# Second-half router logits taken from raw residual chunks, rows finished on three engines, one-step SiLU gate

## The reference, cut to what matters

```
x = x + g1 * mixed
h2 = rms_norm(x, norm2_g) * (1 + sc2) + sh2
g_logits = hf @ w_rg + b_rg                       # 4 groups
e_logits = (hf @ w_re + b_re)                     # 32 experts, hf = h2 in f32
... top-1 group, top-2 experts in it, softmax gates
(jax.nn.silu(xb @ w1[e]) * (xb @ w3[e])) @ w2[e]  # per expert, rows gathered from h2
x = x + g2 * y;  y = rms_norm(x, final_norm_g)
```

## Time and profile before

| what | value |
|---|---|
| median of 3 runs | 1680.51 us (1679.48 to 1683.24) |
| the profiled execution's own time | 1682.7 us |
| its span, first to last instruction | 1680.9 us |
| PE busy | 95% of the span |
| DVE busy / ACT busy | 75% / 48% |

### The profile page before, as it was taken

One profiled execution on the slowest core, in us unless ns is written; L12 is line 12 of the kernel. 1 busy time (PEld: TensorE's weight loads), 2 busy tenths in 40 slices (PEclk: granted clock), 3 DMA queues, 4 the chain that ended last, 5 costly groups with the idle time before them and its releaser, 6 DMA issues.

```text
span 1680.9 us, 23712 instructions
## 1 busy us (share of the span) xinstructions
PE 1600.2 (95%) x9358; PEld 1377.5 (82%) x9358; DVE 1262.6 (75%) x1699; ACT 804.7 (48%) x875; POOL 235.1 (14%) x231
## 2 busy tenths in 40 slices
PE   5999999999999999999999988999999999999953
PEld 3777788788789999999999987888888888888841
DVE  4668886746838798877444268989999899899838
ACT  4222232234333213222242444878878878788723
POOL 0310000000000000002001111354321211212100
PEclk9999999999999999999999998999999999999977
DMA  9955222424434232234223457999999999999855
GB/s 338 305 179 175 83 86 83 139 76 147 120 101 151 88 88 70 76 94 133 70 82 112 184 200 225 415 390 402 385 379 377 375 381 380 379 386 397 300 220 198
DMA packets 215761, 368.51 MB, mean 219 GB/s; under 512 B 15110, under 2 KB 163654, under 8 KB 190298
## 3 DMA queue, kind: packets, MB, share of 16 engines
q1 hardware_dynamic: 197724, 327.95, 55.3%
q0 software_dynamic: 17280, 36.89, 6.1%
q10 hardware_dynamic: 646, 2.15, 0.3%
HBM read 353.45 MB, written 31.20 MB: 229 GB/s over the span
## 4 chain that ended last, share of the span: by engine, by line
PE 86%; DVE 7%; DMA 2%; DVEq 2%; ACT 1%; issue 1%; SPq 1%; POOLq 0%; ACTq 0%
PE z L2426 15%; PE z L2428 15%; PE z L2427 15%; PE z L723 7%; PE z L725 7%; PE z L724 7%; PE z L740 4%; PE z L741 4%; PE z L742 4%; PE q L714 2%; PE q L2319 1%; DMA w_raw<-in_w_in_dram 1%; PE q L731 1%; SPq L1226 1%; DVE conv L1917 1%
## 5 line engine op out<-in xcount | busy, mean ns | idle before, releaser
L970 DVE TENSOR_TENSOR wl<-wr,whr 128x2048 fp32r<-128x2048 f32 x198 | 444.3, 2285 | 0.0
L2426 PE MATMUL z<-h_hi,w_hi 128*128 128x272 f32 (+1 forms) x1248 | 410.6, 329 | 2.1 <-DVE h_lo L1740 1.2
L2428 PE MATMUL z<-h_hi,w_lo 128*128 128x272 f32 (+1 forms) x1248 | 404.9, 324 | 0.0
L2427 PE MATMUL z<-h_lo,w_hi 128*128 128x272 f32 (+1 forms) x1248 | 404.5, 324 | 0.0
L878 ACT ACTIVATE whr<-wr 128x2048 fp32r<-128x2048 f32 x198 | 376.4, 1914 | 35.8 <-PE z L725 31.5
L1740 DVE TENSOR_TENSOR w_lo<-w_raw,w_hi 128x1024 fp32r<-128x1024 f32 (+1 forms) x168 | 179.5, 1069 | 139.4 <-ACT w_hi L1472 139.4
L2426 PEld LDWEIGHTS z<-h_hi,w_hi 128*128 128x128 f32 x1248 | 236.7, 190 | 31.4 <-issue 12.4
L2428 PEld LDWEIGHTS z<-h_hi,w_lo 128*128 128x128 f32 x1248 | 236.4, 189 | 17.3
L2427 PEld LDWEIGHTS z<-h_lo,w_hi 128*128 128x128 f32 x1248 | 236.8, 190 | 15.9 <-issue 0.2
L723 PE MATMUL z<-whr,xTh 128*128 128x512 f32 x528 | 210.0, 398 | 2.4 <-DVE xTl L970 2.4
L725 PE MATMUL z<-wl,xTh 128*128 128x512 f32 x528 | 207.1, 392 | 0.0
(11 more groups left out here) (378 smaller groups left out, 2216.0 us busy)
## 6 DMA issues: line engine op xcount, KB each, us to landing
wr<-in_w_dram SPq DMA_DIRECT2D x198, 1024.0 KB, 7.9
w_raw<-in_w_in_dram SPq DMA_DIRECT2D x104, 512.0 KB, 3.8
ada<-in_w_ada_dram SPq DMA_DIRECT2D x6, 2048.0 KB, 12.4
w_raw<-in_w_branch_dram SPq DMA_DIRECT2D x48, 256.0 KB, 2.7
w_raw<-in_w_out_dram SPq DMA_DIRECT2D x16, 512.0 KB, 3.7
yin<-y_rows SPq DMA_DIRECT2D x16, 512.0 KB, 9.9
ada_h<-in_w_ada_dram SPq DMA_DIRECT2D x2, 2048.0 KB, 15.2
ada_u<-in_w_ada_dram SPq DMA_DIRECT2D x2, 2048.0 KB, 9.9
```

Of the source, the lines that this page charges most:

```text
L970: return dve.tensor_tensor(out, a, b, op)
L2426: pe.matmul(out, w_hi[w][:, k, :], hi[:, k, t0:t1], start=(k == 0), stop=False)
L2427: pe.matmul(out, w_hi[w][:, k, :], lo[:, k, t0:t1], start=False, stop=False)
L2428: last = pe.matmul(out, w_lo[w][:, k, :], hi[:, k, t0:t1], start=False, stop=(k == kn - 1))
```

## The change

- The second half's logits no longer come from the finished rows. With x the residual, A and B scale and shift, r the root: logits = r * ((x*A) @ W) + B @ W + bias. In the output stage PE transposes each residual chunk as it is (`x1_columns`), ACT scales it by A's column while copying (`x1_read`), PE multiplies with the router weights as the stationary operand, 64 wide, even and odd chunks in the two halves of the array's columns (`column_scores`); a second small product adds the halves and turns back to rows (`row_scores`); DVE applies r and adds B @ W + bias (`last_scores`). The first half's logits use the same two products, once for all four tiles (`first_columns`, `first_rows`), after its last transpose.
- A as columns (`abT`) and B @ W + bias (`cbp`, `cbs`) are made in the GB0 stage of the second half: `factor_columns`, `shift_scores`, `shift_rows` on PE, `factors_read`, `shift_read`, `bias_rows` on DVE. Their source is a new DRAM copy of the modulation rows (`modc_dram`), stored by POOL early on with four more DMAs and loaded by POOL into `bn_g`, whose own use is over.
- DVE multiplies each chunk by A into `xA` in the output stage (`x1_scale`). After the root, DVE finishes row tiles 0 and 1 in one pass each; ACT multiplies tiles 2 to 4 by the root, and POOL adds their shift. SP, not POOL, stores the rows. The squares of the last chunk go from ACT to DVE.
- DVE no longer waits for `dense_done` before routing; it waits for POOL's adds ahead of `ohv`. SP loads four expert chunks early, not five.
- The gate is ACT silu and one DVE product.
- One output transpose moves into the middle of the last item; `last_transpose`, `last_logits`, and 44 idle multiplications go.

```diff
@@ PE, second half
-            def logits(t):
-                ...
-                for k in range(KD):
-                    last = pe.matmul(q[s][:, 0, 0:NR], h2T[0][:, k, :], rw[:, k, :], start=(k == 0), stop=(k == KD - 1))
+            def column_scores(out, x, c, first, last):
+                r = 64 * (c % 2)
+                return pe.matmul(out[r:r + NRP], rw[:, c, :], x, start=first, stop=last)
+
+            def row_scores(out, g, t, rows):
+                return pe.matmul(out[0:rows, t * NR:(t + 1) * NR], LT[g][:, t * P:t * P + rows], both[:], start=True, stop=True)
+            def first_columns():
+                ...
+                q_wait_read(pe, "h2T", 0, PT - 1)
+                q_wait_free(pe, "vT", 1, 0)
+                for c in range(KD):
+                    last = column_scores(q[1][:, 0, :], h2T[:, c, :], c, c < 2, c >= KD - 2)
+                last.then_inc(lt_ok, 1)
+            def factor_columns():
+                s = q_wait_free(pe, "mc")
+                pe.wait_ge(mc_in, 32)
+                transposed(q[s][:, 0, 0:P], bn_g[:, 0:P])
+                transposed(q[s][:, 0, P:9 * 2 * KD], bn_g[0:2 * KD, P:2 * P]).then_inc(q_ready[s], 1)
+            def shift_scores():
+                ...
+                for c in range(KD):
+                    last = column_scores(q[s][:, 0, 0:9], abT[:, :, 0, c], c, c < 2, c >= KD - 2)
@@ PE, order of GB0
                 item(g, GB0, h_hi, h_lo)
                 if g:
                     states()
+                    factor_columns()
                 item(g, GB0 + 1, act1_hi, act1_lo, split_ok=blo_ok)
                 pairs(GB0, 1, 3, act1_hi, act1_lo)
+                if g:
+                    shift_scores()
@@ PE, order of the seam
-            for _ in range(44):
-                pe.matmul(z[1][:, 0, 0:P], ident[:], ident[:], start=True, stop=True)
-            for t, rows in tiles(1):
-                last_transpose(t, rows)
-                if t:
-                    last_logits(t - 1, P)
-            last_logits(PT, SMP)
+            x1_columns(0)
+            out_transpose(1, KD // 2 - 1, 1)
+            for c in (1, 2, 3):
+                x1_columns(c)
+            x1_scores(0)
+            x1_columns(4)
+            x1_columns(5)
+            x1_scores(1)
+            x1_columns(6)
+            x1_columns(7)
+            x1_samples()
+            x1_scores(2)
+            x1_scores(3)
+            sample_scores()
+            last_rows()
@@ POOL, second half
                     for n in range(NS):
                         pool.dma_start(new_a_sample[0, n, HA - TS:HA, :], cv[n * TS:(n + 1) * TS, 0:W]).then_inc(st_out, 16)
                         pool.dma_start(new_c_sample[0, n], ot[1][n * TS + TS - HC:(n + 1) * TS, 0:W]).then_inc(st_out, 16)
+                    pool.dma_start(bn_g[:, 0:P], modc_dram[0:P, :]).then_inc(mc_in, 16)
+                    pool.dma_start(bn_g[0:2 * KD, P:2 * P], modc_dram[P:9 * 2 * KD, :]).then_inc(mc_in, 16)
                     pool.wait_ge(v_out, 16)
@@ POOL, moe_gpsimd
-            dense_done(pool)
+            pool.wait_ge(item_mm, 2 * NI)
             pool.memset(xg[0][:], 0.0).then_inc(xg0_ok, 1)
             pool.drain()
+            for t, rows in tiles(1)[NH_D:]:
+                shift = B2[:] if t < PT else xs_s[:, 0:D]
+                pool.wait_ge(hs_ok, t - NH_D + 1)
+                pool.tensor_tensor(h2s[t][0:rows, :], h2s[t][0:rows, :], shift[0:rows, :], ALU.add).then_inc(hp_ok, 1)
+            pool.drain()
+            dense_done(pool)
@@ DVE, the seam
+                    tt(sq7[:, 0:PT, :], xres[:, 0:PT, c], xres[:, 0:PT, c], ALU.mult)
+                    tt(sq7[0:SMP, PT, :], xres[0:SMP, PT, c], xres[0:SMP, PT, c], ALU.mult)
+                    dve.drain()
+                    dve.wait_ge(x1_sq, PT + (KD - 1) * (PT + 1))
+                    dve.tensor_reduce(sp8[:, 0:PT, KD - 1], sq7[:, 0:PT, :], axis=AX.X, op=ALU.add)
+                    dve.tensor_reduce(sp8[0:SMP, PT:PT + 1, KD - 1], sq7[0:SMP, PT:PT + 1, :], axis=AX.X, op=ALU.add)
...
             tail_start(1)
-            for t in range(PT):
-                tail_h2(1, t)
-            dve.wait_ge(abs_in, 16 * 2 * NS)
-            tail_h2(1, PT, SMP, (xs_s[:, D:2 * D], xs_s[:, 0:D]))
-            for t, rows in tiles(1):
-                tail_logits(1, t, rows)
+            dve.wait_ge(h2_out, PT * 16)
+            for t in range(NH_D):
+                dve.scalar_tensor_tensor(h2s[t][:], xA[:, t, :], r2y[:, t:t + 1], B2[:], ALU.mult, ALU.add).then_inc(h2_ok, 1)
+            last_scores()
             moe_vector(dve)
-            dense_done(dve)
             dve.wait_ge(rt_const, N_RT)
...
+            dve.wait_ge(hp_ok, PT + 1 - NH_D)
             for k in range(2):
                 dve.tensor_scalar(ohv[:, k, :, 0, :], oh[:, k], vlo[:, 0:1], None, ALU.mult)
@@ DVE, the gate
-            def gate_one():
-                tt(gs[:], hsg[:], z[0][:, 0, :], ALU.mult).then_inc(m_g1, 1)
-
-            def gate_two():
-                tt(gs[:], gs[:], z[0][:, 1, :], ALU.mult).then_inc(m_g2, 1)
+            def gate():
+                tt(gs[:], hsg[:], z[0][:, 1, :], ALU.mult).then_inc(m_g2, 1)
```

More of the change, by code:

```diff
@@ L1817, in _ @@
             tt(sumw[:], sumw[:], ident[:, 96:105], ALU.add)
+            tt(both[:], ident[:, 0:NR], ident[:, NRP:NRP + NR], ALU.add)
             s = q_wait_ready(dve, "sic")
@@ new lines, in last_scores, with factors_read @@
+            def last_scores():
+                dve.wait_ge(lg_ok, 2)
+                for t, rows in tiles(1):
+                    src, cb = q[1][0:rows, 1, t * NR:(t + 1) * NR], cbp if t < PT else cbs
+                    for out, a, b in ((gpad[0:rows, PT + t, 0:NG], 0, NG), (logit[0:rows, PT + t, :], NG, NR)):
+                        last = dve.scalar_tensor_tensor(out, src[:, a:b], r2y[0:rows, t:t + 1], cb[0:rows, a:b], ALU.mult, ALU.add)
+                last.then_inc(lg_rd, 1)
+            def factors_read():
+                s = q_wait_ready(dve, "mc")
+                dve.tensor_copy(abT[:, :, :, :].rearrange("p n a k -> p (n a k)"), q[s][:, 0, 0:9 * 2 * KD]
+                                ).then_inc(q_free[s], 1)
@@ L2409, in _, with item @@
             pe.wait_ge(xt_free, PT)
-            def item(g, i, hi, lo, split_ok=None):
+            def item(g, i, hi, lo, split_ok=None, between=None):
                 u, s, w, kn = i // 2, i % 2, (NI * g + i) % WS, w_cols(i)
@@ L2419, in item @@
                     [(part, k) for part in parts for k in range(kn)]
-                for (b, t0, t1), k in steps:
+                for n, ((b, t0, t1), k) in enumerate(steps):
+                    if between and n == kn:
+                        between()
                     out = z[s][:, b, 0:t1 - t0]
@@ new lines, in last_rows @@
+            def last_rows():
+                for t, rows in tiles(1):
+                    if t % PT == 0:
+                        pe.wait_ge(ltc_ok, 2 + t // PT)
+                    last = row_scores(q[1][:, 1, :], 1, t, rows)
+                last.then_inc(lg_ok, 1)
+            def factor_columns():
[3 more added lines that the diff above has]
+                transposed(q[s][:, 0, P:9 * 2 * KD], bn_g[0:2 * KD, P:2 * P]).then_inc(q_ready[s], 1)
@@ L2476, in out_item @@
+            def out_item(g, j, s, between=None):
                 i = O0 + 2 * j + s
-                item(g, i, macc_hi, macc_lo, split_ok=mlo_ok if i == O0 else None)
+                item(g, i, macc_hi, macc_lo, split_ok=mlo_ok if i == O0 else None, between=between)
             def out_transpose(g, j, s):
```

394 lines of the change are left out of this document (238 added, 156 removed).

## The result

The changed kernel took 1689.90 us (median of 16 runs, 1688.64 to 1693.95), the kernel before 1681.55 (16 runs, 1678.35 to 1689.20): a ratio of **1.0053, interval 1.0042 to 1.0064**, slower by 0.53%, some 8.4 to 8.9 us. The forecast was 1684.0, so its sign was right and its size less than half of the measured.

The account below looks back on a forecast made before the run. PE was taken as the bound in dense stage and experts, with PE waiting for DVE and the gather at the seam. 13.3 + 1.8 - 0.8 - 14.1 + 3.3 = +3.5 us gave 1684.0 us, range 1679 to 1690.

Parts of the forecast that it names:

- Part 1, the wait: In GB0 PE waits for the two loads into bn_g, issued behind POOL's 18 stores: 13.3 us.
- Part 1, the clock: After the GB0 wait PE resumes at half clock, costing 1.8 us; earlier restarts lost 2.6 and 1.5.
- Part 2: PE's own work in the dense stage, old logits out, new score and row products in: -0.8 us.
- Part 3, the seam: Between the last dense item and the routing, which starts at 983.7 instead of 997.86: -14.1 us.
- Part 3, "the adds beside the routing, no wait": POOL's three adds, with 3.3 us available for each, finish before DVE needs them at `ohv`: no wait.
- POOL's adds are late: Rival: adds over 3.3 us each stop DVE ahead of `ohv`; at 5 us each, 5.1 more, 1689.1; chance 0.16.
- Part 4, the gather: The gather of expert 0's rows, now under full chunk loading, takes 9.1 us instead of 5.82: +3.3 us.
- the turns between queues: Engines alternating queues packet by packet give the gather half the bandwidth, 2.5 us: a term of 1.3.
- Part 5, the gate at nothing: In the experts, DVE's 0.69 us less per block gains nothing, since PE is full.
- three signs of being wrong: GB0 wait under 10 us, POOL's adds over 3.3 us each, or the gather keeping its 5.8.

Follow-up runs that it names:

- e1: The changed kernel with the two loads of modulation columns into bn_g moved ahead of the state stores on POOL's queue: 1676.91 us, ratio 0.9968.
- e5: The changed kernel with 50 identity products on PE ahead of its wait for the column loads in GB0: 1689.32 us, ratio 1.0033.
- e3: The changed kernel with POOL's three adds of 1024 columns cut to one column each: 1688.28 us, ratio 1.0024.
- e6: The changed kernel with each of POOL's three adds cut into eight adds of 128 columns: 1689.26 us, ratio 1.0039.
- e11: The changed kernel with the gate of before (sigmoid, two products) in the experts: 1689.73 us, ratio 1.0056.

## Why the prediction was right in sign and wrong in size

- *Part 1, the wait*: 13.3 forecast, 13.4 measured, from the queue's order alone. Removing it gave 13 to 15 us (e1).
- *Part 1, the clock*: 1.8 was taken, 3.2 measured in this pair of traces. Both rows for it were at hand; the 2.6 of PE's restart in the experts was nearer than the 1.5 of the tail, and I chose the second. But six executions with the same wait lost 1.7, 1.9, 2.8 and three times 3.2: the term was a range of 1.7 to 3.2 and not a number. e5 and the other five traces without the idle wait show that it is the idle wait that brings it.
- *Part 2*: up to the end of the last item -0.3 forecast, -1.0 measured, as what is left over in the table. The eight score products of the first half took 3.65 us for 3.4, where eight at 0.86 one after the other are 6.9, so the two halves of the array do overlap. The row, from the changed kernel:

```profile
562.97 3.65 PE L2544 MATMUL q<-h2T,rw 128*64 128x512 f32 x16
```

- *Part 3, the seam*: counted from the end of the last item, 12.1 us forecast and 13.7 measured; against the kernel before, 1.5 less gained than forecast. The root's sum starts nearly where it was put (5.7 us behind the last output pass, for 5.4); the two passes took 2.5 for 2.3, the logits then waited 0.79 for PE's row products, for which nothing was taken, and took 1.5 for 1.1.
- *Part 3, "the adds beside the routing, no wait"*: **the step that failed**. I looked for the price of POOL's adds in a wait ahead of `ohv`, and put the routing itself at its old length. There was no wait there, as forecast: the adds took 2.3 us each. It was paid 9 us earlier by two DVE instructions that carry no semaphore of POOL's, 2.64 us of the 2.95 by which the routing grew; the other 0.31 is the unexplained pause. The rival *POOL's adds are late* named the shared memory and set its price by POOL's slowness, not by DVE's. e3 and e6 show the mechanism.
- *Part 4, the gather*: +3.3 forecast, +4.0 measured, right in kind and low in size. It missed an edit: chunk 8 is no longer loaded ahead, so nine chunks load there, not eight. The bytes don't explain it by an even share; the turns between queues of the Trainium skill, "DMA: Bandwidth & Descriptors" (Queues, rings and completion order), which were weighed there, gave too low a price as they were applied, 1.3 us for a measured 4.0.
- *Part 5, the gate at nothing*: right (e11).
- *The range* of 1679 to 1690 holds the 1689.9 by a hair, on the side of the rival that shared one cause with the truth. That this rival's 1689.1 came so near is luck: its condition, adds over 3.3 us each, did not hold. None of the three signs of being wrong came either (wait 13.4, adds 2.3, gather 10.0); none of them looked at the routing's own length, where the largest error was.

The errors hardly cancel: the wait +0.1, the clock +1.4, the seam +1.5, the routing +2.95, the gather +0.7, the experts and tail +0.6, less 1.1 at the start and 0.7 in PE's own work, are the 5.4 between 3.5 and 8.9, but for rounding.

## What to carry to other kernels

When a transfer is added for an engine that is the bound, count what stands ahead of it on its own queue: two loads behind 18 stores cost more than the rewrite brought, and moving two lines gave it back. When work is handed to POOL to run beside DVE, look at every DVE instruction in that stretch, not only at those that wait for POOL's result; cut POOL's instructions short, or place them beside work of DVE that reads once. And where a transfer on the path starts amid bulk loads that are wanted much later, hold the loads back.

## What the runs showed of the hardware

- A DVE product of 36 columns went from 0.20 to 2.26 us while POOL added 1024 columns, back to 0.20 with one-column adds, and to 0.36 with the same adds in eight pieces.
- One f32 identity product of 128 by 128 took 0.226 us and stands as two rows in the trace (105 of them: `x210`, 23.71 us).
- PE that idled 13.4 us came back at half of its 2.4 GHz for 6 us (3.2 lost; 1.7 to 3.2 in six executions); with the wait filled by products, or gone, it went on at full clock in six of six. The clock also dipped between 800 and 840 us in all twelve, with PE busy throughout.
- A gather of 0.5 MB took 5.6 to 6.1 us from issue to T(0) in four traces with the bulk loads held back, and 10.0 to 10.8 in seven with the DMA engines full, in one of them though the loads went on for 5 us more.
- The same 1.4 us of idle PE at 985 us was followed by full clock in one execution and by 20 us of half clock in another, worth 7 us in the trace.
